# RWKV-7 heads split over the two partition halves, a shorter router chain, and a weight load ahead of a state store

## The reference, cut to what matters

```python
# first recurrence (RWKV-7), 8 heads of 64, per token
sa = einsum('bhij,bhj->bhi', S, a_t)
S  = S * w_t + sa (x) b_t + v_t (x) k_t
y  = einsum('bhij,bhj->bhi', S, r_t)
# second recurrence: gated DeltaNet, 4 heads of 128, in chunks of 64
# router: best of 4 groups, then the best 2 of its 8 experts
gp, gidx = top_k(softmax(x @ router_g + b_g), 1)
ev, eidx = top_k(elog[gidx], 2)
wts = gp * softmax(ev)
# experts: y += gate[:, e] * (silu(x @ wg) * (x @ wu)) @ wd, 32 experts
```

## Time and profile before

| | us |
|---|---|
| median of 3 runs (904.42 to 909.98) | 906.2 |
| the profiled execution | 905.59 |
| its span, first to last instruction | 903.7 |
| PE busy | 872.6 (97%) |
| DVE busy | 364.2 (40%) |
| ACT busy | 180.6 (20%) |
| POOL busy | 35.3 (4%) |

### The profile page before, as it was taken

How to read it: one execution, slowest core, us unless ns; L and a number is a source line. 1 busy time by engine, 2 the same in 40 slices (tenths; PEclk the granted TensorE clock), 3 DMA queues, 4 the chain that set the end, 5 groups by cost and what they waited for, 6 DMA issues and landing times.

```text
span 903.7 us, 13649 instructions
## 1 busy us (share of the span) xinstructions
PE 872.6 (97%) x5520; PEld 525.0 (58%) x5520; DVE 364.2 (40%) x848; ACT 180.6 (20%) x361; POOL 35.3 (4%) x92
## 2 busy tenths in 40 slices
PE   9999999998999999969999999999999999999996
PEld 7667767785677667765455435543554355435543
DVE  6476999783579483250022012201220122012204
ACT  3341001346221320131111111111111111111112
POOL 0002304200100000000000000000000000000000
PEclk9999999999999999989999999999999999999999
DMA  7333273104534327934999999999999999999951
GB/s 274 94 95 115 77 176 101 56 8 124 180 105 137 115 87 302 379 130 160 405 421 429 416 415 413 429 418 415 416 428 418 416 416 429 417 410 418 429 239 54
DMA packets 36789, 247.68 MB, mean 274 GB/s; under 512 B 12048, under 2 KB 14224, under 8 KB 24208
## 3 DMA queue, kind: packets, MB, share of 16 engines
q1 hardware_dynamic: 36752, 247.17, 69.5%
HBM read 242.23 MB, written 4.92 MB: 273 GB/s over the span
## 4 chain that ended last, share of the span: by engine, by line
PE 88%; DMA 4%; DVE 4%; ACT 2%; issue 1%; SPq 0%; DVEq 0%; ACTq 0%
PE psum L1109 37%; PE psum L563 11%; PE psum L1064 7%; PE psum L1144 7%; PE psum L574 6%; PE psum L1021 4%; DMA sb_arena<-w_gab 2%; PE psum L872 2%; DMA sb_arena<-w_in 2%; PE psum L992 1%; PE psum L1068 1%; PE psum L1127 1%; DMA sb_arena<-w_oab 1%; PE psum L738 1%; PE psum L715 1%
## 5 line engine op out<-in xcount | busy, mean ns | idle before, releaser
L1109 PE MATMUL psum<-sb_arena 128*64 128x512 f32 x1536 | 334.0, 593 | 2.4 <-ACT sb_arena L1437 1.4
L1109 PEld LDWEIGHTS psum<-sb_arena 128*64 128x64 f32 x1536 | 110.7, 136 | 213.6 <-issue 213.6
L2109 DVE TENSOR_TENSOR sb_arena<-sb_arena,psum 128x512 f32<-128x512 f32 x16 | 11.0, 688 | 305.0 <-PE psum L1109 305.0
L563 PE MATMUL psum<-sb_arena 128*128 128x313 f32 (+2 forms) x480 | 127.5, 424 | 1.3 <-DMA sb_arena<-w_in 1.3
L563 PEld LDWEIGHTS psum<-sb_arena 128*128 128x128 f32 x480 | 90.0, 190 | 36.3 <-DMA sb_arena<-w_in 2.9
L2104 DVE TENSOR_TENSOR sb_arena<-sb_arena,psum 128x288 f32<-128x288 f32 x120 | 54.5, 454 | 74.8 <-PE psum L1144 71.0
L1064 PEld LDWEIGHTS psum<-sb_arena 128*128 128x128 f32 x544 | 64.9, 199 | 14.5 <-issue 14.5
L574 PE MATMUL psum<-sb_arena 128*128 128x288 f32 x256 | 68.4, 419 | 4.5 <-DMA sb_arena<-w_gab 4.5
L1064 PE MATMUL psum<-sb_arena 128*128 128x128 f32 x544 | 68.1, 285 | 1.4 <-DVE sb_arena L2053 1.4
L1144 PE MATMUL psum<-sb_arena 128*128 128x288 f32 x240 | 61.3, 407 | 0.0
L574 PEld LDWEIGHTS psum<-sb_arena 128*128 128x128 f32 x256 | 47.7, 192 | 22.3 <-DMA sb_arena<-w_gab 6.7
(11 more groups left out here) (380 smaller groups left out, 769.6 us busy)
## 6 DMA issues: line engine op xcount, KB each, us to landing
sb_arena<-w_gu SPq DMA_DIRECT2D x64, 2048.0 KB, 15.0
sb_arena<-w_dn SPq DMA_DIRECT2D x32, 2048.0 KB, 10.9
sb_arena<-w_in SPq DMA_DIRECT2D x30, 512.0 KB, 3.6
sb_arena<-w_gab SPq DMA_DIRECT2D x16, 512.0 KB, 3.9
sb_arena<-w_oab SPq DMA_DIRECT2D x16, 256.0 KB, 3.4
sb_arena<-gdn_in SPq DMA_DIRECT2D x4, 512.0 KB, 4.9
sb_arena<-w_o SPq DMA_DIRECT2D x4, 512.0 KB, 6.2
sb_arena<-w_o SPq DMA_DIRECT2D x1, 2048.0 KB, 8.0
```

Of the source, the lines that this page charges most:

```text
L563: last = mm(bk(n % 2, N)[:, first_col(n):], w_ring[n % 2][:, k, :], (xw if n < 2 else xnT)[:, k, first_col(n):], start=(k == 0), stop=(k = ...
L1109: last = mm(bank[b][half, :], rows[:, k, half], weights(s, k), start=(k == 0), stop=(k == n_k - 1))
```

## The change

- The state of the first recurrence is stored head by head: `SWr` and `STr` have 64 columns where they had 128, with the even head on partitions 0 to 63 and the odd head on 64 to 127, and no zeros. Loads and stores of it run over 128 partitions in long runs. POOL's three fills are gone, and with them the waits for `z_dead` 3.
- Right-hand side: 8 matmuls of 64 x 64 from `STr`, each on its own head's half, then 8 from `SV`; bank 2 now holds the even heads on partitions 0 to 63 and the odd on 64 to 127, 256 columns, and so does `Rs`. The inverse of the odd heads is copied to partitions 64 to 127 by ACT (one new copy, `xt_up`, before chunk 0), and the product with it goes to banks 1 and 3. `start_states` has 64 matmuls for the first recurrence instead of 32. Chunk 0's permutation has 4 matmuls of 256 columns.
- DVE: one instruction of 128 x 256 where there were two of 64 x 256.
- SP: gate tile 2 is loaded in front of the store of `wkv_s`, gate tile 3 behind it, and both stores of states are one DMA each.
- Router: the logits are folded before the tokens are turned; the counts are 5 matmuls instead of 9; three loops over the 3 token tiles in DVE become one instruction each; one step of the group search is fused; slots count from 1, so one step on them goes; two fills move ahead; ACT signals after every copy to `xe`, and the first matmul of the first expert starts after the first copy, in an order of k that follows the copies.

```diff
-        SW = at(proj_at, NSEQ, T4, P)
+        SWr = at(proj_at, NSEQ, T4, C)
+        SW = at(proj_at, NSEQ, T4, P)
...
-            sp.wait_ge(S["z_dead"], 3)
+            sp.wait_ge(S["z_dead"], 1)
             for piece in range(4):
                 load_in(20 + piece, 21 + piece)
-                sp.dma_start(SW[rows_, b:b + 4, :, par_ * C:par_ * C + C], dram["wkv_in"][rows_, b:b + 4])...
+                sp.dma_start(SWr[:, b:b + 2], dram["wkv_in"][:, b:b + 2]).then_inc(S["ld_sw"], 16)
...
-            for par_, rows_ in halves:
-                sp.dma_start(dram["wkv_p"][rows_], STr[rows_, (NC - 1) % 2, :, par_ * C:par_ * C + C]).then_inc(S["stores"], 16)
+            sp.dma_start(dram["wkv_p"], STr[:, (NC - 1) % 2]).then_inc(S["stores"], 16)
             sp.wait_ge(S["sm_sb"], NSEQ)
             sp.wait_ge(S["ch_y_sb"], NC)
-            sp.wait_ge(S["stores"], 16 * 4)
-            sp.sem_inc(S["rwkv_over"], 1)
-            for par_, rows_ in halves:
-                sp.dma_start(dram["wkv_s"][rows_], SW[rows_, :, :, par_ * C:par_ * C + C]).then_inc(S["stores"], 16)
-            load_in(GB_T + 2, GB_T + 4)
-            sp.wait_ge(S["stores"], 16 * 6)
+            sp.wait_ge(S["stores"], 16 * 3)
+            sp.sem_inc(S["rwkv_over"], 1)
+            load_in(GB_T + 2, GB_T + 3)
+            sp.dma_start(dram["wkv_s"], SWr).then_inc(S["stores"], 16)
+            load_in(GB_T + 3, GB_T + 4)
+            sp.wait_ge(S["stores"], 16 * 4)
...
+                        if name == "r":
+                            for p_, own_ in halves:
+                                last = mm(bank[4 + 2 * p_ + b // 4][rows_, t * C:t * C + C], starts[own_, t, b, :], SWr[own_, b, t, :],
+                                          start=True, stop=True)
+                            continue
...
+                for t in range(T4 if c else 0):
+                    for p_, rows_ in halves:
+                        mm(bank[2][rows_, t * C:t * C + C], AR[rows_, t, c, 0, :], STr[rows_, (c - 1) % 2, t, :], start=(t == 0), stop=False)
+                if c == 0:
+                    for g in range(2):
+                        for p_, rows_ in halves:
+                            first = C0r[:, g].rearrange("p (t q c) -> p t q c", t=T4, q=2)[:, :, p_, :]
+                            mm(bank[2][rows_, 0:T4 * C], perm[:, g, 0, :], first, start=(g == 0), stop=False)
                 for t in range(T4):
...
+                    for p_, rows_ in halves:
+                        h = 2 * t + p_
+                        last = mm(bank[2][rows_, t * C:t * C + C], GM[:, c, h, 0:C], SV[:, c, h * C:h * C + C], start=False, stop=(t == T4 - 1))
...
-                for h in range(HR):
-                    last = mm(bank[3][0:C, h * C:h * C + C], XTr[0:C, c, h, :], Rs[0:C, h * C:h * C + C], start=True, stop=True)
+                for t in range(T4):
+                    for p_, rows_ in halves:
+                        last = mm(bank[1 + 2 * p_][0:C, t * C:t * C + C], XTr[rows_, c, 2 * t + p_, :], Rs[rows_, t * C:t * C + C],
+                                  start=True, stop=True)
...
-            for m in range(3):
-                for q in range(m + 1):
-                    last = mm(bank[6][:, m * E:m * E + E], K("ones" if q < m else "before" if m < 2 else "before_in"), member[:, q, :],
-                              start=(q == 0), stop=(q == m))
-            for m in range(3):
-                last = mm(bank[6][:, 3 * E:4 * E], K("ones"), member[:, m, :], start=(m == 0), stop=(m == 2))
+            mm(bank[6][:, 0:2 * E], K("before"), member[:, 0:2, :], start=True, stop=False)
+            mm(bank[6][:, 2 * E:3 * E], K("before_in"), member[:, 2, :], start=False, stop=False)
+            mm(bank[6][:, E:3 * E], K("ones"), over(member[:, 0, :], 2), start=False, stop=False)
+            mm(bank[6][:, 2 * E:3 * E], K("ones"), member[:, 1, :], start=False, stop=True)
+            last = mm(bk(7, 3 * E), K("ones"), member.rearrange("p m e -> p (m e)"), start=True, stop=True)
...
+            act.wait_ge(S["inv_out"], 2)
+            A(XTr[C:P, :, 1::2, :].rearrange("p c h i -> p (c h) i"), XTr[0:C, :, 1::2, :].rearrange("p c h i -> p (c h) i"), ACT.Copy).then_inc(S["xt_up"], 1)
...
-                A(Rs[0:C, :], bank[2][0:C, :], ACT.Copy).then_inc(S["ch_rhs_sb"], 1)
+                A(Rs[:, 0:T4 * C], bank[2][:, 0:T4 * C], ACT.Copy).then_inc(S["ch_rhs_sb"], 1)
...
-                        ins = A(xe[:, q::4, :], bk(2 + q, 2, P), ACT.Copy)
-                    ins.then_inc(S["xe"], 1)
+                        A(xe[:, q::4, :], bk(2 + q, 2, P), ACT.Copy).then_inc(S["xe"], 1)
...
-                for p_, rows_ in halves:
-                    v = SW[rows_, n - 1, :, p_ * C:p_ * C + C]
-                    last = TT(v, v, bk(6 + n % 2, T4, P)[rows_, :, p_ * C:p_ * C + C], ALU.add)
+                TT(SWr[:, n - 1], SWr[:, n - 1], bk(6 + n % 2, T4, C), ALU.add).then_inc(S["sm_sb"], 1)
...
-            for m in range(3):
-                last = TT(taken[:, m].rearrange("p (g e) -> p g e", g=G), spread(ohg[:, m], EG), over(ev[:, m], G), ALU.mult)
-            step(last)
+            step(TT(taken.rearrange("p m (g e) -> p m g e", g=G), spread(ohg, EG), ev.unsqueeze(2).to_broadcast([P, 3, G, EG]), ALU.mult))
...
-            step(TS(slot[:, :, 0:E], slot[:, :, 0:E], -1.0, None, ALU.add))
```

More of the change, by code:

```diff
@@ L1031, in _ @@
             last.then_inc(S["rms_mm"], 1)
+            pe.wait_ge(S["rt_sb"], 1)
+            for q in range(3):
+                last = mm(bank[6][:, q * 36:q * 36 + 36], logitsT[:, q * P:q * P + P], K("fold"), start=(q == 0), stop=(q == 2))
+            last.then_inc(S["rt_mm"], 1)
             for m in range(3):
@@ L1102, in sparse, with project @@
             def sparse():
-                def project(b, n_k, rows, weights):
-                    for k in range(n_k):
+                def project(b, n_k, rows, weights, order=None):
+                    for at_, k in enumerate(order or range(n_k)):
+                        if order and at_ % 2 == 0:
+                            pe.wait_ge(S["xe"], at_ // 2 + 1)
                         for s in range(2):
                             half = slice(s * CAP, s * CAP + CAP)
-                            last = mm(bank[b][half, :], rows[:, k, half], weights(s, k), start=(k == 0), stop=(k == n_k - 1))
+                            last = mm(bank[b][half, :], rows[:, k, half], weights(s, k), start=(at_ == 0), stop=(at_ == n_k - 1))
                     return last
@@ L1761, in _ @@
             dve.wait_ge(S["sm_mm"], 1)
-            for p_, rows_ in halves:
-                last = CP(STr[rows_, 0, :, p_ * C:p_ * C + C], bk(6, T4, P)[rows_, :, p_ * C:p_ * C + C])
-            last.then_inc(S["ch_st_sb"], 1)
+            CP(STr[:, 0], bk(6, T4, C)).then_inc(S["ch_st_sb"], 1)
             mask_r(2)
@@ L1770, in _ @@
                 dve.wait_ge(S["ch_y"], c)
-                for p_, rows_ in halves:
-                    half = slice(p_ * C, p_ * C + C)
-                    TT(STr[rows_, c % 2, :, half], STr[rows_, (c - 1) % 2, :, half], spread(PTs[rows_, :, c], C), ALU.mult)
+                TT(STr[:, c % 2], STr[:, (c - 1) % 2], spread(PTs[:, :, c], C), ALU.mult)
                 decay_r(2 * c - 1)
@@ L1779, in _ @@
                 dve.wait_ge(S["ch_st"], c)
-                for p_, rows_ in halves:
-                    v = STr[rows_, c % 2, :, p_ * C:p_ * C + C]
-                    last = TT(v, v, bk(4, T4, P)[rows_, :, p_ * C:p_ * C + C], ALU.add)
-                last.then_inc(S["ch_st_sb"], 1)
+                TT(STr[:, c % 2], STr[:, c % 2], bk(4, T4, C), ALU.add).then_inc(S["ch_st_sb"], 1)
                 sample_r(2 * c)
@@ L1993, in _ @@
             add_square(KD - 1).then_inc(S["rms_sq"], 1)
+            V.memset(slot, 0.0)
+            V.memset(gate, 0.0)
             dve.wait_ge(S["rms_root"], 3)
@@ L2013, in _ @@
             step(TT(rt4, gl, spread(gm, G), ALU.subtract))
-            first_of(ohg, gl, gm, K("first8")[:, EG - G:], G)
-            for m in range(3):
-                last = TT(rte[:, m], el[:, m], spread(ohg[:, m], EG), ALU.mult)
-            step(last)
+            step(STT(ohg, rt4, 0.0, over(K("first8")[:, EG - G:], 3), ALU.is_equal, ALU.mult))
+            step(V.tensor_reduce(tmp, ohg, AX.X, ALU.max))
+            step(TT(ohg, ohg, spread(tmp, G), ALU.is_equal))
+            step(TT(rte, el, spread(ohg, EG), ALU.mult))
             step(V.tensor_reduce(ev, rte.rearrange("p m g e -> p m e g"), AX.X, ALU.add))
@@ L2027, in _ @@
             step(TT(ev, oh1, oh2, ALU.add))
-            for m in range(3):
-                last = TT(taken[:, m].rearrange("p (g e) -> p g e", g=G), spread(ohg[:, m], EG), over(ev[:, m], G), ALU.mult)
-            step(last)
+            step(TT(taken.rearrange("p m (g e) -> p m g e", g=G), spread(ohg, EG), ev.unsqueeze(2).to_broadcast([P, 3, G, EG]), ALU.mult))
             TT(member, taken, spread(K("valid"), E), ALU.mult).then_inc(S["rt_member"], 1)
```

(11 more changed lines are left out.)

62 lines of the change are left out of this document (21 added, 41 removed).

## The result

| | before | after |
|---|---|---|
| median of the runs timed together, us | 907.31 (904.42 to 910.08) | 897.72 (895.34 to 899.19) |
| profiled execution, us | 905.59 | 895.34 |
| its span | 903.7 | 893.6 |
| mean granted clock | 0.991 | 0.987 |
| DMA packets under 512 bytes | 12048 | 3312 |

The ratio is 0.9888 (95% interval 0.9865 to 0.9911). The forecast was 890.5, range 885.5 to 897.0: the kernel is faster, as said, but the number lies 0.7 us over the top of the range. The gain is 9.6 us where 15.6 were summed.

What follows compares the result with a forecast made beforehand. TensorE (PE) was taken to hold nearly all the chain of waits. 4.4 + 0.15 + 5.8 + 2.8 + 0.9 + 1.5 = 15.55 us off 905.59 gave 890.0, stated as 890.5 for the median; range 885.5 to 897.

Steps and rivals of the forecast that it cites:

- the clock in the router: Router: clock still falls, but the earlier gather spends half its time at the low level; gain 1.5 us of 0 to 2.9.
- Chunks 1 to 4: First recurrence: smaller matmuls on alternating array halves cut a chunk from 6.2 to 5.1 us, saving 4.4 us over four.
- The rival of small tiles that don't overlap: First recurrence and start states: new 64 x 64 records cost 72 ns each, kernel at 901 us; chance 0.08.
- a changed order of shapes: Recurrence chunks: two more changes between 128 x 64 and 64 x 64 tiles per chunk, charged nothing.
- Start states: Before chunk 0: `start_states` grows from 64 records in 1.89 us to 128, costing plus 1.0 us (range 0.9 to 1.9).
- Chunk 0: First chunk: PE's blocks shrink, but PE waits for DVE's first mask behind unmoved convolutions, so only 0.15 us arrives.
- The store behind the load: Behind the first recurrence: loading gate tile 2 before the state store removes 4.21 us wait and 1.6 of clock, 5.8 us.
- Router: Path to the gather: fewer steps on the way to `member` and 5 count matmuls start the gather 2.8 us sooner.
- Signals of `xe`: Router to first expert: signals after each copy start the first expert about three copies earlier, 0.9 us.
- The end: Behind the router: expert rounds keep their program and only move; nothing charged for the kernel's end.
- a drain that the sum had never charged: Recurrence: TensorE draining at tiling changes; at 0.2 us each, eight more would cost 1.6 us, but nothing was charged.
- the inverse at its dear end: Chunks 1 to 4: the inverse stays at 1.16 us instead of 0.61, so the four chunks save 2.2 us.

Runs made afterwards that it cites:

- e3: Changed kernel with five of the first gate tile's units moved into PE's wait for DVE's first mask: 893.23 us, ratio 0.9861.
- e1: Kernel before with only gate tile 2's load issued ahead of the first recurrence's state store: 902.79 us, ratio 0.9968.
- e6: Changed kernel with the state store again issued ahead of gate tile 2's load, new state layout kept: 895.35 us, ratio 0.9888.
- e7: Kernel before with 24 never-executed matmuls at the head of the dense branch: 908.61 us, ratio 1.0036.
- e2: Changed kernel with 16 never-executed matmuls at the head of the dense branch: 891.92 us, ratio 0.9844.
- e9: Second run of e3's kernel (changed kernel, five gate units moved into the mask wait), a single execution: 894.12 us.
- e5: The changed kernel unaltered, timed again: 896.27 us, ratio 0.9894 to the kernel before.
- e4: Changed kernel with six and two matmuls whose results nobody reads, where PE waits in the router: 888.81 us, ratio 0.9814.
- e10: Kernel of e8 with DVE's steps for `gate` moved behind the slots, selection and flag: 884.51 us, ratio 0.9760.
- e11: Kernel of e8 unaltered, run again: 885.57 us, ratio 0.9765.
- e12: Kernel of e10 with four gate units (33, 34, 41, 42) moved forward between the small matmuls behind the recurrence: 884.73 us, ratio 0.9748.
- e8: Kernel of e4 with gate units 2 to 7 in chunk 0's mask wait and gate tile 2's load issued during the recurrence: 886.22 us, ratio 0.9787.

## Why the prediction was wrong, and where it was right

The step that failed is in the prediction's treatment of what comes behind the router: "The expert rounds keep their program and only move." It let the end of the kernel move with them and charged it nothing; it cost 3.7 us. The second failed term is the clock in the router, 1.5 us, of which 0.3 came in the profiled execution. Term by term:

- **Chunks 1 to 4, 4.4 us: right.** 4.99 us a chunk against 5.1 said and 6.2 before. From chunk 1's start to the end of the recurrence it is 20.7 us (196.71 - 175.97) where it was 24.95 (201.10 - 176.15), 4.2; the rest stayed in chunk 1, whose first blocks ran at half the clock. The inverse in two banks costs 0.68 on its own as a block, as the alternating halves of L758 did. The rival of small tiles that don't overlap is out, and a changed order of shapes cost nothing that can be seen.
- **Start states, plus 1.0: wrong by its sign.** The 128 records take 1.48 us (L659, from 159.19), where the 64 before took 1.89. I had priced them from records of 22 and 30 ns, but on alternating row halves they take 12 ns each (1.48 / 128), which fits two running at once. It lay under cover.
- **Chunk 0, 0.15 us: right by two errors.** "Nothing in the change moves the convolutions" failed: DVE's first mask came at 172.77 instead of 173.69. PE was 1.5 us ahead before any touched matmul (L688 at 155.97, L686 before at 157.49). Nearly all of it arose between 95 and 145 us, where PE takes 49.00 us for the same 192 records that took 50.36: its waits for input weights at 115.82 and 124.71, which stood beside the state loads in short runs, are gone. (The idle times of 0.39 and 0.44 us understate them, since neighbouring records overlap when there is no wait.) The waits stand in all three profiles with the old layout and in none of the eleven with the new. Before, in the timeline:

```profile
115.82 8.45 PE L563 MATMUL psum<-sb_arena 128*128 128x304 f32 x32 [0.39 <-DMA sb_arena<-w_in]
124.71 5.64 PE L563 MATMUL psum<-sb_arena 128*128 128x304 f32 x21 [0.44 <-DMA sb_arena<-w_in]
```

After, one run of records without a wait:

```profile
109.72 20.63 PE L561 MATMUL psum<-sb_arena 128*128 128x304 f32 x80
```

  I named these quicker loads and wrote them off against the wait for the mask, which itself moved. So the mask and PE came 0.9 us sooner. Against this stands the clock: PE now stands 2.81 us there, the clock fell, and only 0.18 us was left at chunk 1's start (175.97, before 176.15). That 0.15 had been said is luck. e3 shows what the fall and the unit behind it cost, 1.3 us.
- **The store behind the load, 5.8: right in size, wrong in cause.** The wait of 4.21 us went but for some 0.4 us, the clock stays at 1.00 behind the recurrence, and from there on the kernel is 10.2 to 10.5 us ahead (10.35 were summed). But e1 and e6 show that it was the layout of the store and not the order of the queue. Nor does the load move alone for 4.0 us, as the prediction has it: the store is issued 0.38 us behind it, and it takes 4.77. That PE asks for tile 3 some 6 us later would not have saved the case with the old store: in e1 it asks, and waits 2.51 us.
- **Router, 2.8 us: 2.2.** At the start of the last L1012 (L1003 before) the kernel was 10.46 us ahead, at the gather 12.63. To the first count it gained 0.90 of the 1.07 that were summed, from there to the gather 1.27 of 1.73. I had set DVE's `gate` steps as the bound for the slots; by the rows the counts ended later, since they ran at half the clock (2.45 us, where I had 1.8 or less).
- **Signals of `xe`, 0.9: right**, 0.83 (1.42 idle became 0.59).
- **The clock in the router, 1.5: failed, 0.3.** I let the fall stand but had the gather spend half its time at the high level. It took 6.42 us. The term was taken from one execution and rests on the moment: with the old router the gather took 6.71, 5.53 (e1) and 5.18 us (e7), with the new one 6.42, 6.65 (e2, e6, e9), 6.53 (e3) and 5.16 (e5). So a sooner start of the work does not bring the high level sooner, and a right number here would have been luck. Without the fall the gather takes 3.81 us, and e4 puts the whole price of that clock at 3.4 us.
- **The end, 0: this is the term that was missing.** A stall of 3.04 us and a low clock behind it, 3.7 us in all. It has nothing to do with any edit as such, only with where PE's instructions lie (e2, e7). Without it the median would have been near 894, inside the range.
- **The range.** Its own bounds don't add up. The lower one, 887.5, takes off a drain that the sum had never charged (with the clock kept high alone it is 889.1); the upper one, with the inverse at its dear end and no gain of clock, is 890.5 + 2.2 + 1.5 = 894.2 and not 893.5. Neither would have let the result in.

As a sum, in the profiled executions: 15.55 - 0.6 (router) - 1.2 (its clock) = 13.75, which the expert rounds show (13.77); less 3.7 is 10.1, the difference of the spans. The small misses of the other terms cancel.

## What to carry to other kernels

- Where a kernel takes a branch near its end, look at the first us behind it for an "issue" wait of 2 to 3 us, and pad the program that isn't run: two lines gave 0.4% here. Before crediting an edit with so small a change, check that the place of the code has not made it.
- A long wait of PE was charged twice here, for itself and for the clock behind it (waits of 2.24, 2.51, 2.81, 3.04, 3.54 and 4.21 us). Real work moved into it (e3), or matmuls that nobody reads (e4), buy the second part back. When an edit shortens PE's side of a meeting with another engine, it opens such a wait.
- An exchange in a queue and the layout of what is queued should be tried apart: e1 and e6 cost two runs and reversed the explanation.

## What the runs showed of the hardware that was not expected

- Code that isn't executed changes the time: +3.3 us (e7), -3.7 (e2). The stall ended 2.9 to 3.5 us after the first record behind the branch, whether it began behind record 1, 2 or 46.
- 128 records of 64 rows by 32 columns took 1.48 us, 12 ns each, at the high clock.
- The granted clock fell from 2.4 to 1.2 GHz with no long wait of PE just ahead of it, behind 2.9 us of blocks on few rows, in five profiles (e3, e9, e10, e11, and e1, where a wait of 2.51 us lay 6 us back) and behind the second group of them in e12. It did not fall in eight: the kernel before, the changed kernel, e2, e4, e5, e6, e7 and e8. e8 is the same program as e11 and reached the blocks 0.4 us sooner.
